# One-hot rows a block ahead of the low parts, two sets of banks for the second products, and a later wait for the last gate store

## The chip, the cores and the metric

One core of a Trainium2 chip runs the kernel. The time is that of one execution on the device in microseconds (us): 2182.56 us, the median of three runs (2181.74 to 2182.63). One more execution was profiled; its own time is 2186.8 us, and the stretch from its first to its last instruction, the span, is 2185.0 us. Times in a trace count from the start of the span.

Engines: TensorE (PE, and PEld for its weight loads), VectorE (DVE), ScalarE (ACT), GpSimd (POOL), and SyncE (SP), which only issues DMAs. Each engine runs its own instructions in their order and waits for the others by semaphores.

## The reference

The program is one layer of an encoder on 512 tokens of width 1024, in float32. Its first half (attention, a convolution, gates, an output projection, a norm) is not touched by the change. The second half, which takes the last two thirds of the time, looks each token up in a table of 16384 single-neuron experts:

```python
q = (hf @ w_q).reshape(T, PEER_HEADS, 2, PEER_DHALF)
scores = jnp.einsum('thpd,pnd->thpn', q, sub_keys)        # 2 x 128 keys for each of 8 heads
sv, si = lax.top_k(scores, 16)
cand = sv[:, :, 0, :, None] + sv[:, :, 1, None, :]
cv, ci = lax.top_k(cand, 16)                               # 16 experts a head: 128 a token
e_idx = si_0[ia] * N_KEYS + si_1[ib]
gates = softmax(cv)
a = einsum('thkd,td->thk', u_tab[e_idx], x)
out = einsum('thk,thkd->td', gelu(a) * gates, v_tab[e_idx])
x = layer_norm(ALPHA * x + (1 + g2) * out, ln2_g, ln2_b)
```

## The kernel before

The experts form a square of 128 x 128 keys. For three of the four token tiles (384 tokens, `TN`) the kernel doesn't gather; it computes all experts: 128 blocks of 128 experts, one block for each first key.
**First products** (`first_product(c)`, L1711 and on). Block c is 24 matrix products of 128 x 384 columns into bank 0 or 1. Its table block `raw` (128 x 1024 floats) is loaded by SP (`load_u`), four buffers. ScalarE copies it to the high part `whi` (L743, in `ahead`, together with the GELU of the block before, L750); three buffers, so the high part of block c+2 waits for the end of block c-1. VectorE subtracts to get the low part `wlo` (`low_u`, L1192), two blocks ahead of its use; for every third block GpSimd does that (L552, `on_pool`). The GELU results `gelz` go to DRAM four blocks at a time (SP), since the weights aren't known yet.

**Beside them.** `select(t)` on VectorE finds the top 16 for tile t; it takes 18 blocks. Then `laying`, 16 blocks a tile, for the three tiles 1 to 3, turns the choices into gates by key: for eight tokens at a time VectorE makes two sets of one-hot rows, `one` (128 slots x 8 tokens x 128 keys each): L1328 compares the first keys with an iota, L1330 the second keys, L1332 multiplies by the softmax weights. TensorE multiplies the two (`token_gates`, L1748, four tokens in a bank, two such steps a block, each ahead of half of the block's products), ScalarE copies the result to `stage` (L766) and every eight steps stores 128 x 4096 floats to DRAM (`gates_by_key`). `one` has two buffers; the rows of step o wait until the gates of step o-2 are done (`gt_mm`). In between VectorE takes the dot products of the gathered tile (`dot`, L1197: `ring` with `x2s`). In the order of the blocks: selection 0 (blocks 0 to 17), selection 1 (to 35), selection 2 (to 53), laying 1 (54 to 69), selection 3 (70 to 87), laying 2 (88 to 103), laying 3 (104 to 119), and a fill stage of eight blocks (120 to 127). In the trace the three laying stages are 779 to 958, 1059 to 1232 and 1233 to 1420 us.

**The fill stage.** Before block 120's part ScalarE waits until all gates are stored (`stage_out`) and issues two loads of gates (`gring`) and three of GELU results (`gback`). From its fifth step on (j = 4) the weights gate x GELU are formed (`weigh`, L1359, VectorE), split (`eh` L812 on ScalarE, `el` L1365 on VectorE), and the rows of the second table are split (`vhi` L824, `vlo` L1371).

**Second products** (`second_product`, L1776 and on). 16 groups of eight blocks; each group once for each half of the 1024 output columns. For each block and each of the three tiles three products of 512 columns are summed in a bank over the eight blocks of the group, and then VectorE adds the sum to `acc` in SBUF (`add`, L1387 and L1389). All half groups use the same banks 2, 3 and 4: the first product of a half group into a bank waits (`pv_add`) until the last sum was read from it. VectorE's low parts `vlo` run three blocks ahead of TensorE, in four buffers. In groups 0 to 5 VectorE also takes dots. Group 6 sets up the gathered tile's weights, by a transpose through bank 5, and in groups 7 to 14 the "quads" (L1802) multiply them with 128 gathered rows of the second table, into banks 6 and 7. The last group writes the gate row of the norm into banks 0 and 1, and VectorE carries out the residual, the norm and the output.

The steps named below are in these functions:

## Time and profile before

| | |
|---|---|
| median of the runs | 2182.56 us |
| the profiled execution, its own time | 2186.8 us |
| its span | 2185.0 us |
| TensorE busy | 1766.1 us, 81% of the span |
| VectorE busy | 1439.6 us, 66% |
| ScalarE busy | 732.3 us, 34% |
| GpSimd busy | 517.4 us, 24% |
| mean granted clock of TensorE | 0.904 of full speed |
| DMA | 441.12 MB, mean 202 GB/s |

The shares are means over stages that have different limits. TensorE has by far the most work, so its idle time is looked at first, by the waits that end it and by stage; then what the engine that it waits for was itself waiting for. "<-" in a row names what was waited for, and the number in brackets at the end of a row of the timeline is the idle time just before it. The granted clock is 1.0 where TensorE runs at 2.4 GHz and 0.5 where it runs at 1.2 GHz. A DMA share is the mean busy share of the 16 DMA engines.

### The profile page before, as it was taken

The page shows a single profiled execution, that of the slowest core. Times are in us where ns is not written, and L with a number is a line of the kernel's source. Part 1 is how long each engine was busy: PE and PEld are TensorE (multiplying, and loading weights), DVE is VectorE, ACT ScalarE, POOL GpSimd, SP SyncE. Part 2 cuts the span into 40 slices and gives each one's busy share as a digit, 9 for nine tenths or more (in the row PEclk, how much of TensorE's full clock was granted, in tenths as well). Part 3 has the DMA queues.
Part 4 walks back from the last instruction along what each step waited for, and adds up shares of the span by engine and source line. Part 5 has one row for each costly group of instructions (what it writes and reads, how often), then busy time and mean ns, then how long its engine had stood idle before and what let it go on. Part 6 is the DMA issues. An engine that isn't in the chain of part 4 may idle for free. (4 is left out here: it accounts for less than half of the span.)

```text
span 2185.0 us, 23650 instructions
## 1 busy us (share of the span) xinstructions
PE 1766.1 (81%) x8496; PEld 1482.6 (68%) x8496; DVE 1439.6 (66%) x2735; ACT 732.3 (34%) x1068; POOL 517.4 (24%) x386
## 2 busy tenths in 40 slices
PE   4997799879989865688665656678988898999985
PEld 3885567669989865688665656677766765566664
DVE  6349998856999954569544444448787654454458
ACT  4433354243323323333233323323333322232232
POOL 1019800020222211112211111123223022343321
PEclk9998899979999988889788778799999998999998
DMA  7242235514465535455335333398888689899982
GB/s 280 68 145 78 78 116 192 174 69 145 165 245 205 176 126 187 149 183 198 121 149 202 141 139 139 130 328 307 288 287 289 217 285 332 311 359 340 348 282 102
DMA packets 177972, 441.12 MB, mean 202 GB/s; under 512 B 15552, under 2 KB 64832, under 8 KB 176320
## 3 DMA queue, kind: packets, MB, share of 16 engines
q1 hardware_dynamic: 78992, 224.62, 29.5%
q0 software_dynamic: 38256, 139.48, 18.1%
q10 hardware_dynamic: 60608, 75.50, 10.1%
q8 instruction: 69, 1.13, 0.2%
q14 instruction: 47, 0.39, 0.0%
HBM read 384.99 MB, written 54.53 MB: 201 GB/s over the span
## 5 line engine op out<-in xcount | busy, mean ns | idle before, releaser
L1516 PE MATMUL bank<-act_hi,whi 128*128 128x384 f32 (+1 forms) x1352 | 504.5, 373 | 39.3 <-DVE wlo L1192 26.1
L1517 PE MATMUL bank<-act_lo,whi 128*128 128x384 f32 (+1 forms) x1352 | 487.2, 360 | 0.0
L1518 PE MATMUL bank<-act_hi,wlo 128*128 128x384 f32 (+1 forms) x1352 | 485.6, 359 | 0.0
L1516 PE MATMUL bank<-vhi,eh 128*128 128x512 f32 x768 | 317.0, 413 | 73.3 <-DVE acc L1389 39.3
L1192 DVE TENSOR_TENSOR wlo<-raw,whi 128x1024 fp32r<-128x1024 f32 x87 | 109.2, 1258 | 321.2 <-ACT whi L743 320.1
L1516 PEld LDWEIGHTS bank<-act_hi,whi 128*128 128x128 f32 x1352 | 270.7, 200 | 60.4 <-DVE wlo L1192 30.3
L1517 PE MATMUL bank<-vlo,eh 128*128 128x512 f32 x768 | 310.1, 404 | 0.0
L1518 PE MATMUL bank<-vhi,el 128*128 128x512 f32 x768 | 308.9, 402 | 0.0
L1371 DVE TENSOR_TENSOR vlo<-vraw,vhi 128x512 fp32r<-128x512 f32 x256 | 175.1, 692 | 200.9 <-ACT vhi L824 174.3
L1748 PE MATMUL bank<-one 128*128 128x128 f32 x768 | 135.3, 333 | 208.7 <-DVE one L1332 208.7
L1517 PEld LDWEIGHTS bank<-act_lo,whi 128*128 128x128 f32 x1352 | 268.9, 199 | 12.3
L1518 PEld LDWEIGHTS bank<-act_hi,wlo 128*128 128x128 f32 x1352 | 266.5, 197 | 13.4
L1748 PEld LDWEIGHTS bank<-one 128*128 128x128 f32 x768 | 124.5, 239 | 219.2 <-DVE one L1332 219.2
L824 ACT ACTIVATE vhi<-vraw 128x512 fp32r<-128x512 f32 x256 | 158.7, 628 | 299.0 <-PE bank L1518 152.5
L544 POOL DMA_INDIRECT ring<-in_u_tab_dram,idxN x128 | 145.1, 1133 | 438.0 <-DVE ring L1197 423.7
L1516 PEld LDWEIGHTS bank<-vhi,eh 128*128 128x128 f32 x768 | 150.3, 196 | 140.5 <-issue 76.3
L552 POOL TENSOR_TENSOR wlo<-raw,whi 128x1024 fp32r<-128x1024 f32 x41 | 100.0, 2439 | 515.8 <-ACT whi L743 515.5
L766 ACT ACTIVATE stage<-bank 128x512 f32<-128x512 f32 x96 | 106.2, 1106 | 341.7 <-PE bank L1748 341.7
L567 POOL DMA_INDIRECT ring<-in_v_tab_dram,idxT x128 | 132.9, 1038 | 328.8 <-PE bank L1802 268.9
L1518 PEld LDWEIGHTS bank<-vhi,el 128*128 128x128 f32 x768 | 150.4, 196 | 33.7
L1517 PEld LDWEIGHTS bank<-vlo,eh 128*128 128x128 f32 x768 | 150.9, 197 | 30.4 <-issue 0.2
L750 ACT ACTIVATE gelz<-bank 128x384 f32<-128x384 f32 x128 | 62.9, 491 | 297.9 <-PE bank L1518 277.6
(222 smaller groups left out, 2359.0 us busy)
## 6 DMA issues: line engine op xcount, KB each, us to landing
raw<-in_u_t_dram SPq DMA_DIRECT2D x128, 512.0 KB
vraw<-in_v_tab_dram SPq DMA_DIRECT2D x256, 256.0 KB
raw<-in_wblk_dram SPq DMA_DIRECT2D x61, 512.0 KB, 4.2
raw<-in_w_modt_dram SPq DMA_DIRECT2D x48, 512.0 KB, 3.5
gelu_ahead<-gelz SPq DMA_DIRECT2D x32, 768.0 KB
gates_by_key<-stage ACTq DMA_DIRECT2D x12, 2048.0 KB
gring<-gates_by_key ACTq DMA_DIRECT2D x32, 768.0 KB
gback<-gelu_ahead ACTq DMA_DIRECT2D x64, 384.0 KB
```

The source lines that it names most:

```text
L544: pool.indirect_dma_start(out=ring[:, j % RING, :], out_offset=None, in_=u_tab, in_offset=bass.IndirectOffsetOnAxis(ap=idxN[:, j:j + 1], a ...
L552: nc.gpsimd.tensor_tensor(wlo[:, c % SPL, :], raw[:, c % RAW, :], whi[:, c % SPL, :].bitcast(F32), ALU.subtract).then_inc(u_lo_pool, 1)
L567: pool.indirect_dma_start(out=ring[:, n % RING, :], out_offset=None, in_=v_tab, in_offset=bass.IndirectOffsetOnAxis(ap=idxT[:, tok:tok + 1 ...
L750: nc.scalar.activation(gelz[:, c % PS, :], bank[c % 2][:, 0:TN], ACT.Gelu_apprx_tanh).then_inc(gel_r, 1)
L766: nc.scalar.activation(stage[:, s, :, t0:t0 + TOK].rearrange("p i t -> p t i"), bank[2 + b % 2][:, :].rearrange("p (t i) -> p t i", t=TOK) ...
L824: nc.scalar.activation(hi_slot, vraw[:, n % VR, :], ACT.Copy).then_inc(v_hi, 1)
L1192: nc.vector.tensor_tensor(wlo[:, c % SPL, :], raw[:, c % RAW, :], whi[:, c % SPL, :].bitcast(F32), ALU.subtract).then_inc(u_lo, 1)
L1371: nc.vector.tensor_tensor(lo_slot, vraw[:, n % VR, :], hi_slot.bitcast(F32), ALU.subtract).then_inc(v_lo, 1)
L1516: mm(o, wh, mh, start=start, stop=False)
L1517: mm(o, wh, ml, start=False, stop=False)
L1518: return mm(o, wl, mh, start=False, stop=stop)
L1748: last = mm(bank[2 + b % 2][:, j * NK:(j + 1) * NK], row[:, 0, i, :], row[:, 1, i, :], start=True, stop=True)
```

## The change

In `laying` on VectorE the one-hot rows of step o+1 are made before the low part of block c0+o+2 (before: those of step o, after it); the rows of the first step are made ahead of the loop. The second half of each group sums in banks 0, 1 and 5 instead of 2, 3 and 4, so that each sum may be read while the next half group runs; the waits `pv_add` look one half group further back, and the first use of banks 0 and 1 waits for the last GELU. The transpose of group 6 goes through bank 6. In the last group the gate row comes one product later and waits for the sums in banks 0 and 1 to be read. The five loads of ScalarE in the fill stage, with the wait for the stores, come after its third step.

```diff
--- before.py
+++ after.py
@@ -350,6 +350,7 @@
             return (whi0, wlo0) if n == 0 else (whi[:, n % SPL, :], wlo[:, n % SPL, :])
 
         Y_BANK = (0, 2, 6, 4)
+        PV_BANK = ((2, 3, 4), (0, 1, 5))
 
 
         TILES = list(range(V0)) + list(range(C0, Y0))
@@ -824,14 +825,15 @@
                 nc.scalar.activation(hi_slot, vraw[:, n % VR, :], ACT.Copy).then_inc(v_hi, 1)
 
 
-            for i in range(2):
-                act.wait_ge(stage_out[i], 16 * (NTB // 2))
-            for i in range(2):
-                load_g(i)
-            for i in range(3):
-                load_back(i)
             for j in range(FILL):
                 ahead(CH - FILL + j)
+                if j == 2:
+                    for i in range(2):
+                        act.wait_ge(stage_out[i], 16 * (NTB // 2))
+                    for i in range(2):
+                        load_g(i)
+                    for i in range(3):
+                        load_back(i)
                 if j >= 4:
                     part_w(j - 4, j - 4)
                 if j >= 5:
@@ -1315,22 +1317,28 @@
                 link(nc.vector.tensor_copy(selT[:, 0:2, :], selI[:]))
                 nc.vector.nop().then_inc(selT_sb, 1)
 
-            def one_hots(t, c0):
+            def one_hots(t, o):
 
                 shape = [P, WIDE, NK]
+                n = P // WIDE * (t - 1) + o
+                need(dve, gt_mm, 2 * n - 2)
+                row = one[o % 2]
+                part = slice(o * WIDE, (o + 1) * WIDE)
+                keys_of = iota[:].unsqueeze(1).broadcast_to(shape)
+                link(nc.vector.tensor_tensor(row[:, 1], selT[:, 0, part].unsqueeze(2).broadcast_to(shape), keys_of,
+                                             ALU.is_equal))
+                nc.vector.tensor_tensor(row[:, 0], selT[:, 1, part].unsqueeze(2).broadcast_to(shape), keys_of,
+                                        ALU.is_equal)
+                nc.vector.tensor_tensor(row[:, 1], row[:, 1], selT[:, 2, part].unsqueeze(2).broadcast_to(shape),
+                                        ALU.mult).then_inc(one_r, 1)
+
+            def laying(t, c0):
+
+                one_hots(t, 0)
                 for o in range(P // WIDE):
+                    if o + 1 < P // WIDE:
+                        one_hots(t, o + 1)
                     low_u(c0 + o + 2)
-                    n = P // WIDE * (t - 1) + o
-                    need(dve, gt_mm, 2 * n - 2)
-                    row = one[o % 2]
-                    part = slice(o * WIDE, (o + 1) * WIDE)
-                    keys_of = iota[:].unsqueeze(1).broadcast_to(shape)
-                    link(nc.vector.tensor_tensor(row[:, 1], selT[:, 0, part].unsqueeze(2).broadcast_to(shape), keys_of,
-                                                 ALU.is_equal))
-                    nc.vector.tensor_tensor(row[:, 0], selT[:, 1, part].unsqueeze(2).broadcast_to(shape), keys_of,
-                                            ALU.is_equal)
-                    nc.vector.tensor_tensor(row[:, 1], row[:, 1], selT[:, 2, part].unsqueeze(2).broadcast_to(shape),
-                                            ALU.mult).then_inc(one_r, 1)
                     dot(next(dots))
 
             low_u(0)
@@ -1343,10 +1351,10 @@
                 select(t, c0)
                 c0 += PRE_S
                 if t > 1:
-                    one_hots(t - 1, c0)
+                    laying(t - 1, c0)
                     c0 += PRE_L
                 transposed(t)
-            one_hots(TT - 1, c0)
+            laying(TT - 1, c0)
 
             def weigh(g, k):
 
@@ -1383,10 +1391,11 @@
                     wait_sum(g, half, t)
                     need(dve, pv_add, 2 * TD * g + TD * half + t - 2 * TD + 1)
                     dst = acc[:, t, half * HALF:(half + 1) * HALF]
+                    src = bank[PV_BANK[half][t]][:, :]
                     if first:
-                        nc.vector.tensor_copy(dst, bank[2 + t][:, :]).then_inc(pv_add, 1)
+                        nc.vector.tensor_copy(dst, src).then_inc(pv_add, 1)
                     else:
-                        nc.vector.tensor_tensor(dst, dst, bank[2 + t][:, :], ALU.add).then_inc(pv_add, 1)
+                        nc.vector.tensor_tensor(dst, dst, src, ALU.add).then_inc(pv_add, 1)
 
             def residual(t, half):
 
@@ -1400,7 +1409,7 @@
 
                 cut = slice(half * HALF, (half + 1) * HALF)
                 wait_sum(NG - 1, half, t)
-                nc.vector.tensor_tensor(acc[:, t, cut], bank[2 + t][:, :], rows2[:, 0, cut],
+                nc.vector.tensor_tensor(acc[:, t, cut], bank[PV_BANK[half][t]][:, :], rows2[:, 0, cut],
                                         ALU.mult).then_inc(pv_add, 1)
 
             def last_sum(t, half):
@@ -1429,7 +1438,7 @@
                     if last and k == 0:
                         dve.wait_ge(w_mul, CH)
                         diagonals(dg2, 40)
-                    if last and k == 2:
+                    if last and k == 3:
                         gate_row(rows2[:, 0, :], 0, 2)
                         dve.wait_ge(x1_in, 32)
                         dve.wait_ge(g_row, 2)
@@ -1465,7 +1474,7 @@
                                                 iota[:, 0:QUAD].unsqueeze(1).broadcast_to([P, QUAD, QUAD]),
                                                 ALU.is_equal)
                         dve.wait_ge(wT_mm, 1)
-                        link(nc.vector.tensor_copy(wT[:], bank[5][:, 0:P]))
+                        link(nc.vector.tensor_copy(wT[:], bank[6][:, 0:P]))
                     if g == W_GROUP and k in (1, 3, 5, 7):
                         part = slice(k // 2 * QUAD, (k // 2 + 1) * QUAD)
                         nc.vector.tensor_tensor(wz[:, part, :], wT[:, part].unsqueeze(2).broadcast_to([P, QUAD, QUAD]),
@@ -1780,11 +1789,13 @@
                 n = half * GR + k
                 pe.wait_ge(v_lo, 16 * g + n + 1)
                 pe.wait_ge(w_lo, GR * g + k + 1)
+                if g == 0 and k == 0 and half == 1:
+                    pe.wait_ge(gel_r, CH)
                 for t in range(TD):
                     if k == 0:
-                        need(pe, pv_add, 2 * TD * g + TD * half + t - TD + 1)
+                        need(pe, pv_add, 2 * TD * (g - 1) + TD * half + t + 1)
                     c = slice(t * P, (t + 1) * P)
-                    last = three(bank[2 + t][:, :], eh[:, k, c], el[:, k, c], vhi[:, n % VR, :], vlo[:, n % VR, :],
+                    last = three(bank[PV_BANK[half][t]][:, :], eh[:, k, c], el[:, k, c], vhi[:, n % VR, :], vlo[:, n % VR, :],
                                  k == 0, k == GR - 1)
                     if k == GR - 1 and t < TD - 1:
                         last.then_inc(pv_mm, 1)
@@ -1808,11 +1819,12 @@
                 at = V_GROUP <= g < V_GROUP + QUAD // 4
                 for k in range(GR):
                     second_product(g, k, 0)
-                    if last and k == 1:
+                    if last and k == 2:
+                        pe.wait_ge(pv_add, 2 * TD * g)
                         gate_row(dg2, 0, 2)
                     if g == W_GROUP and k == 6:
                         pe.wait_ge(own_w, 1)
-                        nc.tensor.transpose(bank[5][:, 0:P], own_a[:], ident[:]).then_inc(wT_mm, 1)
+                        nc.tensor.transpose(bank[6][:, 0:P], own_a[:], ident[:]).then_inc(wT_mm, 1)
                     if at and k % 4 == 3:
                         quad(4 * (g - V_GROUP) + k // 4)
                 if not last:
@@ -1825,14 +1837,15 @@
                 group(g, g == NG - 1)
 
             g = NG - 1
+            pe.wait_ge(g_row, 2)
             for t in range(TD):
                 c = slice(t * P, (t + 1) * P)
-                need(pe, pv_add, 2 * TD * g + TD + t - TD + 1)
+                pe.wait_ge(pv_add, 2 * TD * (g - 1) + TD + t + 1)
                 for k in range(GR):
                     if t == 0:
                         pe.wait_ge(v_lo, 16 * g + GR + k + 1)
                     h, l = v_slot(GR + k, True)
-                    ins = three(bank[2 + t][:, :], eh[:, k, c], el[:, k, c], h, l, k == 0, k == GR - 1)
+                    ins = three(bank[PV_BANK[1][t]][:, :], eh[:, k, c], el[:, k, c], h, l, k == 0, k == GR - 1)
                 ins.then_inc(pv_mm, 1)
```

On VectorE in the first laying stage, from its first step on, before (`one0_86` and `one1_87` are the two buffers of the one-hot rows; `waits u_hi` is the wait for a high part, `waits gt_mm` that for gates; where no `wlo` stands between two steps, GpSimd makes it):

```order
L1328 TENSOR_TENSOR one0_86<-selT_85,iota_109 128x1024
L1330 TENSOR_TENSOR one0_86<-selT_85,iota_109 128x1024 [waits dch]
L1332 TENSOR_TENSOR one0_86<-one0_86,selT_85 128x1024
L1197 SCALAR_TENSOR_TENSOR ring_88,own_a_123<-ring_88,x2s_81 128x1024 [waits ug_in0]
L1192 TENSOR_TENSOR wlo_53<-raw_51,whi_52 128x1024 [waits u_hi]
L1328 TENSOR_TENSOR one1_87<-selT_85,iota_109 128x1024
L1330 TENSOR_TENSOR one1_87<-selT_85,iota_109 128x1024 [waits dch]
L1332 TENSOR_TENSOR one1_87<-one1_87,selT_85 128x1024
L1197 SCALAR_TENSOR_TENSOR ring_88,own_a_123<-ring_88,x2s_81 128x1024 [waits ug_in1]
L1192 TENSOR_TENSOR wlo_53<-raw_51,whi_52 128x1024 [waits u_hi]
L1328 TENSOR_TENSOR one0_86<-selT_85,iota_109 128x1024 [waits gt_mm]
```

And now, at the same place:

```order
L1328 TENSOR_TENSOR one0_86<-selT_85,iota_109 128x1024
L1330 TENSOR_TENSOR one0_86<-selT_85,iota_109 128x1024 [waits dch]
L1332 TENSOR_TENSOR one0_86<-one0_86,selT_85 128x1024
L1328 TENSOR_TENSOR one1_87<-selT_85,iota_109 128x1024
L1330 TENSOR_TENSOR one1_87<-selT_85,iota_109 128x1024 [waits dch]
L1332 TENSOR_TENSOR one1_87<-one1_87,selT_85 128x1024
L1199 SCALAR_TENSOR_TENSOR ring_88,own_a_123<-ring_88,x2s_81 128x1024 [waits ug_in0]
L1328 TENSOR_TENSOR one0_86<-selT_85,iota_109 128x1024 [waits gt_mm]
L1330 TENSOR_TENSOR one0_86<-selT_85,iota_109 128x1024 [waits dch]
L1332 TENSOR_TENSOR one0_86<-one0_86,selT_85 128x1024
L1194 TENSOR_TENSOR wlo_53<-raw_51,whi_52 128x1024 [waits u_hi]
L1199 SCALAR_TENSOR_TENSOR ring_88,own_a_123<-ring_88,x2s_81 128x1024 [waits ug_in1]
```

The second set of rows has moved ahead of the first dot, and each later set ahead of the low part that stood before the set of the step before; the instructions and their number are the same.

On ScalarE in the fill stage, before (`gelz` with L750 is the GELU of a block, `whi` with L743 a high part):

```order
L800 DMA gring<-gates_by_key 128x12x128 [waits stage_out1,stage_out0]
L800 DMA gring<-gates_by_key 128x12x128
L807 DMA gback<-gelu_ahead 128x768 [waits gel_out0] x2
L807 DMA gback<-gelu_ahead 128x768 [waits gel_out1]
L750 ACTIVATE gelz<-bank 128x384 [waits u_mm]
L743 ACTIVATE whi<-raw 128x1024 [waits u_mm,u_in2]
L750 ACTIVATE gelz<-bank 128x384 [waits gel_out0,u_mm]
L743 ACTIVATE whi<-raw 128x1024 [waits u_mm,u_in3]
```

And now:

```order
L751 ACTIVATE gelz<-bank 128x384 [waits u_mm]
L744 ACTIVATE whi<-raw 128x1024 [waits u_mm,u_in0]
L801 DMA gring<-gates_by_key 128x12x128 [waits stage_out1,stage_out0]
L801 DMA gring<-gates_by_key 128x12x128
L808 DMA gback<-gelu_ahead 128x768 [waits gel_out0] x2
L808 DMA gback<-gelu_ahead 128x768 [waits gel_out1]
L751 ACTIVATE gelz<-bank 128x384 [waits u_mm]
L744 ACTIVATE whi<-raw 128x1024 [waits u_mm,u_in1]
```

The five loads stand behind three GELUs and three high parts that followed them before.

## Rows read from the trace of the kernel before

**Rows 1.** Waits, 773 to 1420.1 us: engine, line <- releaser: us, times, longest
```profile
PE bank L1748 <- DVE one L1332: 208.7, 33, 7.4
```

**Rows 2.** Windows: start:end, us, busy of each engine, PEclk, DMA share, GB/s
```profile
779.20:958.50 179.30, 116.13 (x640) 112.93 (x641) 82.97 (x87) 56.40 (x62) 26.50 (x21) 0.80 0.39 139
1058.60:1232.20 173.60, 110.49 (x601) 107.58 (x602) 81.85 (x85) 54.22 (x60) 26.09 (x20) 0.79 0.37 135
1232.60:1420.20 187.60, 118.16 (x641) 114.97 (x642) 90.10 (x98) 57.64 (x64) 26.08 (x20) 0.79 0.40 147
1420.20:1474.80 54.60, 41.94 (x220) 40.21 (x219) 24.86 (x39) 16.19 (x27) 15.76 (x11) 0.93 0.92 328
1474.80:1751.40 276.60, 239.39 (x982) 192.59 (x983) 213.71 (x364) 96.03 (x167) 64.58 (x48) 0.94 0.82 277
1751.40:2126.30 374.90, 345.97 (x1665) 236.24 (x1665) 180.52 (x306) 109.20 (x192) 120.65 (x120) 0.95 0.93 327
```

**Rows 3.** Timeline of VectorE in laying: start us, us, engine, line, operation, [idle before]
```profile
803.63 1.23 DVE L1192 TENSOR_TENSOR wlo<-raw,whi 128x1024 fp32r<-128x1024 f32 x1 [8.44 <-ACT whi L743]
804.77 1.22 DVE L1328 TENSOR_TENSOR one<-selT,iota 128x1024 f32<-128x1024 f32 x1
...
808.30 1.22 DVE L1197 SCALAR_TENSOR_TENSOR ring<-ring,x2s 128x1024 f32<-128x1024 f32 x1
...
809.44 1.22 DVE L1328 TENSOR_TENSOR one<-selT,iota 128x1024 f32<-128x1024 f32 x1
...
1060.07 1.23 DVE L1192 TENSOR_TENSOR wlo<-raw,whi 128x1024 fp32r<-128x1024 f32 x1 [8.04 <-ACT whi L743]
```

**Rows 4.** Timeline of TensorE: the gate products, eight each, two steps a block
```profile
779.23 2.08 PE L1748 MATMUL bank<-one 128*128 128x128 f32 x8 [5.52 <-DVE one L1332]
...
784.65 1.05 PE L1748 MATMUL bank<-one 128*128 128x128 f32 x8
...
812.99 1.05 PE L1748 MATMUL bank<-one 128*128 128x128 f32 x8
...
815.96 1.05 PE L1748 MATMUL bank<-one 128*128 128x128 f32 x8
...
1238.89 2.08 PE L1748 MATMUL bank<-one 128*128 128x128 f32 x8 [6.34 <-DVE one L1332]
```

**Rows 5.** Timeline of ScalarE in laying
```profile
814.08 1.10 ACT L766 ACTIVATE stage<-bank 128x512 f32<-128x512 f32 x1 [2.44 <-PE bank L1748]
816.16 0.49 ACT L750 ACTIVATE gelz<-bank 128x384 f32<-128x384 f32 x1 [0.98 <-PE bank L1518]
816.55 1.05 ACT L743 ACTIVATE whi<-raw 128x1024 fp32r<-128x1024 f32 x1
```

**Rows 6.** Timelines of GpSimd and VectorE where they meet
```profile
775.47 2.62 POOL L552 TENSOR_TENSOR wlo<-raw,whi 128x1024 fp32r<-128x1024 f32 x1
...
775.81 3.36 DVE L1332 TENSOR_TENSOR one<-one,selT 128x1024 f32<-128x1024 f32 x1
```

**Rows 7.** Timelines of ScalarE's DMA issue and of TensorE in the fill stage
```profile
1427.06 3.94 ACTq L807 DMA_DIRECT2D gback<-gelu_ahead  x3
...
1431.68 0.66 PE L1516 MATMUL bank<-act_hi,whi 128*128 128x384 f32 x1 [7.16 <-ACT gelz L750]
```

**Rows 8.** Waits, 1474.8 to 1751.4 us
```profile
DVE vlo L1371 <- ACT vhi L824: 33.1, 38, 3.3
...
PE bank L1516 <- DVE acc L1389: 23.9, 10, 3.2
...
PE bank L1516 <- DVE acc L1387: 5.8, 2, 4.0
```

**Rows 9.** Waits, 1751.4 to 2130 us, and one DMA issue of ScalarE
```profile
PE bank L1516 <- DVE vlo L1371: 20.9, 5, 5.3
...
PE bank L1516 <- DVE acc L1389: 15.4, 4, 7.5
...
1797.77 6.57 ACTq L807 DMA_DIRECT2D gback<-gelu_ahead  x1
```

## The prediction

> **What bounds the kernel now.** I read the waits first, then busy time by stretch, then the order of time on the engines that meet there. The table of waits between 773 and 1420.1 us has one entry that matters for TensorE: the token gates (L1748) waited 208.7 us, 33 times, for the one-hot rows (L1332) [rows 1]. So in the three laying stages TensorE is the engine waited for by ScalarE, and VectorE is what holds TensorE. VectorE itself is not full there, so the stages run in a ring and not at the pace of any engine. The windows say it: laying takes 179.3, 173.6 and 187.6 us, TensorE is busy 116.1, 110.5 and 118.2 us of it, VectorE 83.0, 81.9 and 90.1, at a granted clock near 0.8 and a DMA share near 0.4 [rows 2]. (The second window begins where TensorE's wait for the first one-hot rows begins, the third with the transposes of the values that it needs.)
>
> The ring can be followed in time. ScalarE takes the GELU of a finished block at 816.16 and makes the next high part at 816.55 [rows 5]. VectorE makes the low part (803.63), and only then the one-hot rows (804.77 to 808.30), then a dot [rows 3]. TensorE can't begin its block before the one-hot rows are there. GELU 0.4 + high part 1.05 + low part 1.14 + one-hot rows 3.53 are 6.1 us, and the wait on record is 6.3 (5.52 to 6.34 in the first waits of the stages) [rows 4, 5]. Only where GpSimd makes the low part (every third block) is there no such wait, since then VectorE goes straight on, at 809.44. After a wait TensorE runs at the lower of its two levels (1.2 instead of 2.4 GHz) for a while: the first half block after 779.23 took 5.42 us to 784.65, one at the full level 2.97 (812.99 to 815.96) [rows 4].
>
> **The laying stages, 48 blocks.** Now the rows of block o+1 are made before the low part of block o+2. They need only the gates of block o-1, which are done in the middle of that block; they are wanted when block o+1 begins. The low part that comes behind them is wanted a block later still. Put on one clock, with TensorE beginning block o-1 at 0 and a block taking 2 x 2.97 = 5.94: its second gates are read by 4.0; one-hot rows of o+1 from 4.0 to 7.6; high part of o+2 at 5.9 + 1.5 = 7.4; low part 7.6 to 8.7; dot to 9.9. The rows are wanted at 11.9 and the low part at 17.8. So neither is late, by 4.3 and 9.1 us, and what is left is throughput. TensorE: 5.94 a block. VectorE: 1.14 + 3.53 + 1.14 = 5.81, or 4.67 where GpSimd makes the low part. ScalarE: GELU 0.4, high part 1.05, two gate copies of 1.1 are 3.65 [rows 5]. TensorE is the bound, closely followed by VectorE.
> - First stage: 16 x 5.94 = 95.0, and 2.4 for the slow start behind the 5.52 us that stay (VectorE is full in the selection before it): 97.4 instead of 179.3, saves 81.9.
> - Second: the first wait goes too, since VectorE is idle 8.04 us ahead of 1060.07 and can make two sets there [rows 3]: 95.0 instead of 173.6, saves 78.6.
> - Third: it starts right behind the transposes of the values. Of 6.34 us the low part's 1.14 goes, 5.2 stay: 102.6 instead of 187.6, saves 85.0.
>
> Sum 245.5. That asks for more DMA: 139 GB/s x 179.3/97.4 = 256 GB/s, by share 0.39 x 1.84 = 0.72 [rows 2]. The queue order of SP is unchanged, but it carries the 512-KB loads of raw (128 x 1024 floats) behind a 768-KB store of gelz every fourth block, and blocks come almost twice as fast. I take 4 us off for single late loads: **241.5**.
>
> The shared port has a price of its own. Where GpSimd's subtraction (2.62 us at 775.47) met VectorE's multiplication (775.81), that took 3.36 instead of 1.22, 2.14 more [rows 6]. Before, most subtractions fell into VectorE's idle time; now VectorE is hardly ever idle. Three blocks cost VectorE 5.81 + 5.81 + 4.67 + 2.14 = 18.43, TensorE 17.82. The excess, 0.6 a triple or 3.3 us in a stage, is inside the 4.3 us that the rows are ahead, so I charge nothing. The Trainium skill (SBUF — State Buffer, "Who interferes with whom") says that a VectorE instruction with two SBUF inputs and a GpSimd instruction that reads SBUF exclude each other for a whole instruction. All five VectorE operations of a block have two such inputs, so by that rule every one of the 16 subtractions is paid; the row at 775.81 agrees with it.
>
> **The last gate store waited for later.** ScalarE now stands still behind block 119: the wait for the store and five DMA issues (three of them 3.94 us from 1427.06) precede the GELU that TensorE waits for, 7.16 us, to 1431.68 [rows 7]. Behind ahead(122) the store has long landed. The issues (5 to 6.6 us for five, going by the 3.94 for three) then delay one high part by 2.5 to 4 us, and its low part is wanted more than a block later. That saves 7.2 + 2 for the slow start. But the weights' first product (at j = 4) now comes some 10 us behind the issue of its operands instead of 20, with the DMA engines at 0.92 of their time [rows 2]. Bounds: -3 (a stall as long as one issue group, less what is hidden) and +9.4. I take **7**, near the upper end, since TensorE has a block in hand there.
>
> **Two sets of sum banks.** Groups 0 to 6 take 276.6 us [rows 2]. TensorE waits 23.9 + 5.8 = 29.7 us for additions in 12 waits [rows 8]; with a second set these waits go. What is late next is VectorE: its order is the same, its low parts run only three products ahead of TensorE, and it is busy 213.7 us of the stretch and waits inside the chain multiply, high part, low part (0.6 a time). All that it could gain are the 33.1 us in which it waits for vhi [rows 8]. So the bounds are 0 and 30. DMA share 0.82 would become 0.88 to 0.92. I take **18**, a bit over half: both engines have to gain it together, and they hand over three products at a time.
>
> Groups 7 to 14 run at a DMA share of 0.93 [rows 2]. There TensorE waits 15.4 us for additions, 20.9 for vlo [rows 9], and the latter stand behind a ScalarE that sat 6.57 us in one DMA issue, 1797.77 [rows 9]. That isn't touched; an addition's wait that goes is mostly taken up by the next of those. Bounds 0 and 22 (15.4 and 4 slow starts of 1.6); I take **5**.
>
> The rest is nothing: bank 6 in the place of 5 for one transpose is unused there (the quads start behind it); gel_r at the first use of banks 0 and 1 was reached a half group ago; in the last group the gate row comes one product later with the same instructions on VectorE, whose chain sets the end either way. 0, bounds -2 and +1.
>
> **Sum.** 241.5 + 7 + 18 + 5 = 271.5. From the profiled execution's 2186.8 (span 2185.0) that is 1915.3; the median of the runs, 2182.6, is 4.2 lower, so 1911.
>
> **Rivals.**
> - *The feed becomes the bound in laying* (0.14). For: behind each 768-KB store the next load is 2 blocks (11.9 us) ahead of its use, with a gate store of 2048 KB (128 x 4096 floats) and 512-KB gathers beside it: 5.2 MB in the worst case, at the 328 GB/s of the fill stage [rows 2] nearly 16 us. 12 such places, 3.6 us each and a slow start of 1.6: 62 us, 1973. Against: a share of 0.72 on the mean, and only 3 of the 4 blocks are loaded late. The Trainium skill (DMA: Bandwidth & Descriptors, "Queues, rings and completion order") has the DMA engines take turns between queue rows packet by packet, so that the load would have at least a third of the rate; by that the 1.3 MB of the store and the load would be through in about 12 us and the stall near nothing. No run here shows the turns.
> - *The shared port sets laying's pace* (0.10), the skill's rule above at full price and the rows' lead used up: 16 x 0.6 = 10 us, 1921.
> - *The second products gain nothing* (0.07), VectorE's chain and DMA taking all: 241.5 + 7 give 1934.
> - *The wait moves from the one-hot rows to the low part* (0.02): the change would not do what it says. It needs the low part 9 us later than reckoned; the other parts alone (7 + 18 + 5) give 2153.
> - *Slower* (0.01): every VectorE operation of laying stretched as at 775.81, by GpSimd's gathers too. It decides from the point where a block costs VectorE more than the present mean, 542/48 = 11.3 us; three of five operations stretched by 2.14 give 12.2, 48 x 0.9 = 43 us more: 2226. Against: the operations of rows 3 took 1.22 us each; the stretched one stands beside a subtraction, and of those there is one in three blocks.
>
> **How the numbers follow.** The forecast has 0.66. Its own range is 1890 to 1935 (30, 22 and 9.4 instead of 18, 5 and 7 below; half of the second part's gain lost and a few late loads above). The range that I give is 1885 to 1960: it takes in the port, the second products and a partly late feed. Two runs of this kernel tell a difference of over 0.2% (4.4 us). Faster 0.98, same 0.01, slower 0.01.
>
> **What would show it.** Right: in laying about 6 us a block, the wait of L1748 for the one-hot rows down to some 11 us in 2 or 3 times, granted clock near 1.0, DMA share near 0.7; no wait for "acc" before the last group, but waits for vlo in its place; TensorE not idle at the start of the fill stage. Wrong: waits of ScalarE's whi for raw in laying (the feed), VectorE at 0.98 of laying with TensorE waiting under 1 us each time (the port), or laying still above 7 us a block.

## The result and the profile after

The changed kernel took 1925.37 us (median of 4 runs, 1920.16 to 1927.09), the kernel before beside it 2182.15 (4 runs, 2181.11 to 2182.63): 0.882 of the time, 95% interval 0.8801 to 0.8839. The forecast was 1911 us, its range 1885 to 1960. The profiled execution took 1926.98 us, its span is 1925.2, 259.8 less than before. One of the runs below, of the kernel with all edits together, took 2796.5 us at a mean granted clock of 0.558 and is left out of its ratio; nothing here tells why.

First the waits of TensorE over the three laying stages of the changed kernel (781 to 1172 us); this answers to [rows 1].

```profile
PE bank L1757 <- DVE one L1332: 17.4, 5, 6.0
...
DVE one L1328 <- PE bank L1757: 6.0, 6, 1.2
...
ACT whi L744 <- DMA raw<-in_u_t_dram: 2.3, 2, 1.3
```

The wait for the one-hot rows fell from 208.7 us in 33 times to 17.4 in 5. Now it is VectorE that waits (6.0 us in all) for gates that TensorE has yet to take, and ScalarE waited only 2.3 us for loads of raw: the feed kept up.

Next the windows of the changed kernel that answer to [rows 2]: laying one to three, fill stage, groups 0 to 6 up to the first quad, first to last quad (start:end, us, busy of each engine, PEclk, DMA share, GB/s).

```profile
781.70:878.50 96.80, 96.77 (x640) 96.60 (x641) 89.99 (x87) 56.34 (x62) 37.32 (x21) 0.98 0.73 257
969.80:1068.60 98.80, 98.42 (x641) 97.94 (x642) 93.25 (x88) 56.50 (x62) 38.68 (x21) 0.97 0.68 251
1074.20:1171.90 97.70, 97.36 (x640) 97.04 (x641) 94.13 (x90) 56.59 (x62) 36.64 (x20) 0.98 0.72 270
1172.00:1225.20 53.20, 41.63 (x221) 39.90 (x219) 24.87 (x39) 16.98 (x29) 14.62 (x11) 0.90 0.98 347
1225.20:1497.80 272.60, 248.11 (x1022) 199.50 (x1024) 217.29 (x372) 96.38 (x171) 59.84 (x48) 0.94 0.83 286
1497.80:1863.20 365.40, 333.21 (x1613) 226.27 (x1612) 173.01 (x294) 105.61 (x186) 119.33 (x120) 0.95 0.93 329
```

In laying TensorE is busy for the whole window, its granted clock went from 0.8 to 0.98, and the DMA share from 0.39 to about 0.7, as forecast. Read from start to start of the stages, the 259.8 us are:

| part | before | after | saved | predicted |
|---|---|---|---|---|
| up to the wait ahead of laying one | 773.7 | 776.3 | -2.6 | 0 |
| laying one | 179.3 | 96.8 | 82.5 | 81.9 |
| laying two, with its first wait | 188.7 | 104.8 | 83.9 | 78.6 |
| laying three, with its first wait | 187.6 | 103.0 | 84.6 | 85.0 |
| fill stage | 54.6 | 53.2 | 1.4 | 7 |
| groups 0 to 6 (up to the first quad) | 287.6 | 272.6 | 15.0 | 18 |
| groups 7 to 14 (first to last quad) | 362.0 | 365.5 | -3.5 | 5 |
| tail | 60.6 | 62.0 | -1.4 | 0 |

What is not in the table (the wait ahead of laying one, and selection 3) took about 91 us in both. The two rows of the groups part at the first quad, which stands four products behind the start of group 7; the prediction's window ended at that start (1751.4 us before, 1481.0 now). Parted there, groups 0 to 6 went from 276.6 to 255.8 us and the rest up to the last quad from 373.0 to 382.3. The difference is one wait: the 7.50 us for an addition that TensorE had ahead of 1751.43 are gone, and 1.03 and 4.55 us for low parts have come inside the first four products of group 7. In either parting the two rows together gained 11.5 us, where the forecast had 23.

A steady block of laying can be read off TensorE's gate products and VectorE's order (timelines of the changed kernel, start us, us, engine, line, operation).

```profile
1008.38 1.05 PE L1757 MATMUL bank<-one 128*128 128x128 f32 x8
1011.35 1.05 PE L1757 MATMUL bank<-one 128*128 128x128 f32 x8
1014.33 1.05 PE L1757 MATMUL bank<-one 128*128 128x128 f32 x8
...
1008.07 1.21 DVE L1328 TENSOR_TENSOR one<-selT,iota 128x1024 f32<-128x1024 f32 x1
1009.32 1.23 DVE L1330 TENSOR_TENSOR one<-selT,iota 128x1024 f32<-128x1024 f32 x1
1010.46 1.22 DVE L1332 TENSOR_TENSOR one<-one,selT 128x1024 f32<-128x1024 f32 x1
1011.60 1.22 DVE L1194 TENSOR_TENSOR wlo<-raw,whi 128x1024 fp32r<-128x1024 f32 x1
1012.73 1.22 DVE L1199 SCALAR_TENSOR_TENSOR ring<-ring,x2s 128x1024 f32<-128x1024 f32 x1
...
1013.88 1.22 DVE L1328 TENSOR_TENSOR one<-selT,iota 128x1024 f32<-128x1024 f32 x1
```

Half a block is 2.97 us on TensorE, a block 5.95; VectorE's round is 5.81, from 1008.07 to 1013.88. Both are the numbers of the forecast.

In the groups, the waits of the changed kernel from 1225.2 to 1497.8 us, and from 1497.8 to 1863.2; they answer to [rows 8] and [rows 9].

```profile
PE bank L1525 <- DVE vlo L1379: 31.0, 9, 6.5
...
DVE vlo L1379 <- ACT vhi L825: 23.2, 29, 3.1
...
PE bank L1525 <- DVE vlo L1379: 32.0, 6, 7.1
...
ACT vhi L825 <- issue: 44.9, 9, 7.8
```

TensorE waits for no addition any more. The last row is ScalarE standing in load issues, 44.9 us in nine times.

### The profile page after: what moved, and what is told of

Same layout as the page of the kernel before. It is cut to its first block and busy times, and to the rows that moved or that the text cites. A ratio compares the mean times of both kernels' runs of the same rounds, so it can differ in the third digit from the quotient of the medians.

```text
span 1925.2 us, 23651 instructions
## 1 busy us (share of the span) xinstructions
PE 1706.1 (89%) x8496; PEld 1431.3 (74%) x8496; DVE 1460.8 (76%) x2735; ACT 730.2 (38%) x1068; POOL 543.0 (28%) x386
## 3 DMA queue, kind: packets, MB, share of 16 engines
q10 hardware_dynamic: 60608, 75.50, 11.5%
## 5 line engine op out<-in xcount | busy, mean ns | idle before, releaser
L1525 PE MATMUL bank<-act_hi,whi 128*128 128x384 f32 (+1 forms) x1352 | 491.1, 363 | 38.2 <-DVE wlo L1194 26.6
L1526 PE MATMUL bank<-act_lo,whi 128*128 128x384 f32 (+1 forms) x1352 | 477.7, 353 | 0.0
L1527 PE MATMUL bank<-act_hi,wlo 128*128 128x384 f32 (+1 forms) x1352 | 477.6, 353 | 0.0
L1525 PE MATMUL bank<-vhi,eh 128*128 128x512 f32 x768 | 316.8, 413 | 66.0 <-DVE vlo L1379 65.8
L1525 PEld LDWEIGHTS bank<-act_hi,whi 128*128 128x128 f32 x1352 | 260.2, 192 | 58.7 <-DVE wlo L1194 30.1
L545 POOL DMA_INDIRECT ring<-in_u_tab_dram,idxN x128 | 166.6, 1302 | 389.9 <-DVE ring L1199 378.0
L1526 PEld LDWEIGHTS bank<-act_lo,whi 128*128 128x128 f32 x1352 | 260.0, 192 | 12.4
L1527 PEld LDWEIGHTS bank<-act_hi,wlo 128*128 128x128 f32 x1352 | 259.3, 192 | 13.2
L553 POOL TENSOR_TENSOR wlo<-raw,whi 128x1024 fp32r<-128x1024 f32 x41 | 106.4, 2594 | 277.9 <-ACT whi L744 277.6
L1199 DVE SCALAR_TENSOR_TENSOR ring<-ring,x2s 128x1024 f32<-128x1024 f32 x128 | 164.4, 1286 | 0.4
L1194 DVE TENSOR_TENSOR wlo<-raw,whi 128x1024 fp32r<-128x1024 f32 x87 | 109.1, 1256 | 48.5 <-ACT whi L744 47.6
L893 DVE TENSOR_TENSOR wlo<-raw,whi 128x1024 fp32r<-128x1024 f32 x61 | 80.0, 1311 | 77.9 <-ACT whi L586 77.9
```

Of the source, the lines that this page charges most:

```text
L545: pool.indirect_dma_start(out=ring[:, j % RING, :], out_offset=None, in_=u_tab, in_offset=bass.IndirectOffsetOnAxis(ap=idxN[:, j:j + 1], a ...
L553: nc.gpsimd.tensor_tensor(wlo[:, c % SPL, :], raw[:, c % RAW, :], whi[:, c % SPL, :].bitcast(F32), ALU.subtract).then_inc(u_lo_pool, 1)
L893: nc.vector.tensor_tensor(low[:, :], raw[:, s % RAW, :], high[:, :].bitcast(F32), ALU.subtract).then_inc(raw_free, 1)
L1194: nc.vector.tensor_tensor(wlo[:, c % SPL, :], raw[:, c % RAW, :], whi[:, c % SPL, :].bitcast(F32), ALU.subtract).then_inc(u_lo, 1)
L1199: nc.vector.scalar_tensor_tensor(out=ring[:, j % RING, :], in0=ring[:, j % RING, :], scalar=1.0, in1=x2s[:], op0=ALU.mult, op1=ALU.mult, a ...
L1525: mm(o, wh, mh, start=start, stop=False)
```

## The experiments

All were timed beside the kernel before on the same chip; its median there was 2182 to 2187 us. The changed kernel's 1925.4 (ratio 0.882, interval 0.8801 to 0.8839) is the measure for those that build on it; of a difference of less than about 0.3% (6 us) the time tells little, and the traces are read. A trace is one execution, and stages in which two kernels are alike differ in it too: the first gates of laying one come between 778.8 and 782.6 us in the kernels that change nothing ahead of them, and first to last quad take 361.3 to 368.3 us in the kernels with the same instructions there.

### Which part brought the time

**The order in laying alone**, on the kernel before:

```diff
+                one_hots(t, 0)
                 for o in range(P // WIDE):
+                    if o + 1 < P // WIDE:
+                        one_hots(t, o + 1)
                     low_u(c0 + o + 2)
-                    (the rows of step o)
                     dot(next(dots))
```

> The kernel before with the new order of laying alone. Theory A (the laying stages give nearly all): the three stages take 97, 105 and 103 us as in the changed kernel, instead of 184.8, 188.7 and 187.6 (waits for the first rows included), so about 251 us less than before: 1931 us, 1927 to 1936. Rival B (the stages gain only because the other edits take load off VectorE or DMA): over 1945 us. The waits of the gate products for the one-hot rows: about 17 us in all, by A.

Measured: 1938.6 us (1929.57 to 1939.64), ratio 0.8865, interval 0.8842 to 0.8888. That is 2.6 us above theory A's range and below B's. In its trace TensorE's first gates of the three stages wait 5.45, 6.02 and 5.20 us, 16.7 in all, as theory A has it.

**All but that**, the changed kernel with laying in the old order:

```diff
-                one_hots(t, 0)
                 for o in range(P // WIDE):
-                    if o + 1 < P // WIDE:
-                        one_hots(t, o + 1)
                     low_u(c0 + o + 2)
+                    (the rows of step o)
```

> The changed kernel with laying in the old order: banks, fill stage and last group are as changed. Theory A: these edits are worth what the two traces differ by behind the laying stages, 1.4 (fill) + 15.0 (groups 0 to 6) - 3.5 (groups 7 to 14) - 1.4 (end) = 11.5 us: 2171 us, 2167 to 2175. The prediction's terms 7 + 18 + 5 would give 30 us: 2152.

Measured: 2171.8 us (2170.77 to 2173.49), ratio 0.9943, interval 0.9925 to 0.9962. Theory A. Against 2183.8 the order alone is worth 245.2 us, the rest alone 12.0, together 257.2; both at once brought 256.8 (2182.15 less 1925.37). So the parts add. The laying sum of the forecast (241.5) holds within 4 us, and the other terms (30 together) came to 12.

**The fill stage's loads at their old place:**

```diff
+            for i in range(2): load_g(i)
+            for i in range(3): load_back(i)
             for j in range(FILL):
-                if j == 2: (the same five loads)
```

> The changed kernel with the five loads and the wait for the gate stores ahead of the fill stage again. Theory A (the stall only moved from block 121 to block 124, since the five issues take 11.1 us when the DMA queues are full): 0 to 3 us slower than the changed kernel, 1926 to 1928. The prediction's term would give 7 us: 1932.

Measured: 1927.64 us (1920.06 to 1930.31), ratio 0.8814, interval 0.8792 to 0.8837. Not to be told from the changed kernel; the 7 us of the forecast are not there. Why, these rows of the changed kernel show (timelines of ScalarE's queue and of TensorE; they answer to [rows 7]).

```profile
1181.94 5.93 ACTq L801 DMA_DIRECT2D gring<-gates_by_key  x2
1187.91 5.21 ACTq L808 DMA_DIRECT2D gback<-gelu_ahead  x3
1193.17 0.49 ACT L751 ACTIVATE gelz<-bank 128x384 f32<-128x384 f32 x1 [10.23 <-issue]
...
1193.81 0.66 PE L1525 MATMUL bank<-act_hi,whi 128*128 128x384 f32 x1 [5.05 <-ACT gelz L751]
```

The five issues held ScalarE for 11.1 us where the forecast had 5 to 6.6. That is more than the block that TensorE had in hand, so the same wait came back later, 5.05 us instead of 7.16. It is the place that made them long: at the old place the same five took 1.17 + 3.94 us before the change (1425.85 and 1427.06), and in this experiment, with everything else as changed,

```profile
1175.63 1.17 ACTq L801 DMA_DIRECT2D gring<-gates_by_key  x2
1176.84 3.99 ACTq L808 DMA_DIRECT2D gback<-gelu_ahead  x3
```

In the changed kernel they come three blocks later and meet SyncE's traffic (a gelz store at 1172.66 and four 512-KB loads of raw issued from 1173.08 on, ahead of the five here; behind them in the experiment, from 1181.81 on): the DMA share is 1.00 from 1172 to 1182 us and 1.03 from 1182 to 1188, against 0.83 from 1172 to 1182 in the experiment. That the full DMA engines are what lengthens an issue fits these numbers; it isn't shown apart from the place.

**One set of sum banks** (shown are the lines of the sums; the reads, the transpose and the last group go back with them):

```diff
-        PV_BANK = ((2, 3, 4), (0, 1, 5))
 ...
-                        need(pe, pv_add, 2 * TD * (g - 1) + TD * half + t + 1)
+                        need(pe, pv_add, 2 * TD * g + TD * half + t - TD + 1)
 ...
-                    last = three(bank[PV_BANK[half][t]][:, :], ...
+                    last = three(bank[2 + t][:, :], ...
```

> The changed kernel with one set of sum banks (and the last group's edits with it) as before. Theory A: the additions' waits come back and the second products lose what they had gained, 15.0 - 3.5 - 1.4 = 10 us: 1935, 1931 to 1940. Rival: the prediction's 18 + 5 = 23 us: 1948. The group period in groups 1 to 5 back from 38.0 to about 40 us.

Measured: 1930.84 us (1928.54 to 1936.05), ratio 0.8839, interval 0.882 to 0.8858. That is at the lower edge of theory A (1931 to 1940) and far from the 1948 of the forecast's terms. The intervals meet, so the time alone doesn't tell this kernel from the changed one, but the traces tell where the bank sets act. From the first second product to the first quad they take 304.8 us here and 285.4 in the changed kernel; from there to the last quad 358.6 and 365.5. (The order in laying alone, which has one set too: 299.6 and 363.4.) So the second set is worth 14 to 19 us up to the first quad. Behind it the 2 to 7 us that it seems to cost lie within what like kernels differ by (361.3 to 368.3): there is surely no gain, and whether there is a cost stays open.

### What limits the groups

In the changed kernel a group of the first seven takes 38.0 us, and TensorE stands once in each, near its beginning; two of these waits:

```profile
1262.69 0.80 PE L1525 MATMUL bank<-vhi,eh 128*128 128x512 f32 x1 [3.04 <-DVE vlo L1379]
1300.63 0.80 PE L1525 MATMUL bank<-vhi,eh 128*128 128x512 f32 x1 [3.44 <-DVE vlo L1379]
```

What VectorE and ScalarE did ahead of the one at 1300.63:

```profile
1295.09 1.88 DVE L1398 TENSOR_TENSOR acc<-acc,bank 128x512 f32<-128x512 f32 x3
1296.88 0.55 DVE L1373 TENSOR_TENSOR el<-wf,eh 128x384 fp32r<-128x384 f32 x1
1297.35 0.55 DVE L1367 TENSOR_TENSOR wf<-gback,gring 128x384 f32<-128x384 f32 x1
1298.49 0.56 DVE L1373 TENSOR_TENSOR el<-wf,eh 128x384 fp32r<-128x384 f32 x1 [0.59 <-ACT eh L813]
1299.88 0.69 DVE L1379 TENSOR_TENSOR vlo<-vraw,vhi 128x512 fp32r<-128x512 f32 x1 [0.84 <-ACT vhi L825]
...
1297.93 0.52 ACT L813 ACTIVATE eh<-wf 128x384 fp32r<-128x384 f32 x1 [2.21 <-DVE wf L1367]
1297.94 0.38 ACTq L801 DMA_DIRECT2D gring<-gates_by_key  x1
1298.41 0.71 ACTq L808 DMA_DIRECT2D gback<-gelu_ahead  x1
1299.22 2.19 ACT L825 ACTIVATE vhi<-vraw 128x512 fp32r<-128x512 f32 x4 [0.77 <-issue]
```

Three additions, two weighings handed to ScalarE and back (0.59 us of idleness each), then two load issues on ScalarE, and only then the high part for which VectorE's low part and so TensorE wait.

**VectorE's load taken away:** dots of groups 0 to 5 over 8 columns.

```diff
-                        dot(next(dots))
+                        dot(next(dots), w=8)
```

> The changed kernel with the dot products of groups 0 to 5 taken over 8 columns instead of the whole row of 2048; the gathers that feed them stay as they are, so most of these dot products is left out and nothing else. In the changed kernel a group of the second half takes 38.0 us (TensorE's waits for the last low part at 1262.69, 1300.63, 1338.62 us), and the question is what sets these 38.0. A (VectorE's chain of low parts, dot product, one-hot sets and adds is full): with about 2.2 us of dot product a step gone, a group falls to where TensorE ends last, at most 35.5 us, and the six groups save 15 us or more: 1905 to 1912 us. B (the loads through the DMA engines, or their issues on ScalarE and GpSimd, set the group): 37.5 to 38.0 us a group and 1922 to 1928 us.

Measured: 1916.92 us (1907.41 to 1918.73), ratio 0.8752, interval 0.8727 to 0.8777. VectorE's busy time between 1260 and 1444 us fell from 150.9 to 115.7 us, but the group only from 38.0 to 36.7 (waits from 1259.70 to 1443.18 in five groups) and the stretch to the first quad from 285.4 to 278.8. Neither theory. (A dot takes 1.22 us on a row of 1024, less than the 2.2 on 2048 that the expectation counts.) VectorE isn't full as an engine, and the loads aren't the limit either, since the next experiment gets far below this with all of them. The chain at the group's start above has no dot in it, and stayed.

**The low parts of the weights one step later**, so that VectorE doesn't wait for ScalarE's answer; ScalarE's high parts of the weights go one step later too, so that it doesn't wait for VectorE's product (ScalarE first, then VectorE):

```diff
-                    if k and not last:
-                        part_w(GR * g + GR + k - 1, k - 1)
+                    if k > 1 and not last:
+                        part_w(GR * g + GR + k - 2, k - 2)
+                if not last:
+                    part_w(GR * g + GR + GR - 2, GR - 2)
 ...
-                        if k < GR - 1:
-                            low_w(g + 1, k - 1)
+                        if k > 1:
+                            low_w(g + 1, k - 2)
```

> The changed kernel with the low part of a chunk in the groups taken one step later behind its high part, on VectorE, so that VectorE no longer waits 0.59 us for ScalarE's high part at each step of a group. A (VectorE's chain sets the group of 38.0 us): 14 waits of 0.59 us, 8.3 us a group at most, of which TensorE's own time lets a part through; 2 to 3 us a group in the first seven groups: 1905 to 1914 us. B (the loads set the group): 1923 to 1928 us. C (the last low part of a group, on which TensorE waits, comes later by the shift): 1930 us or more.

Measured: 1901.68 us (1899.41 to 1903.52), ratio 0.8695, interval 0.8681 to 0.871. Theory A, and 3.3 us more than it gave: the stretch to the first quad is 259.0 us, 26.4 less. VectorE's wait for the weights' high part was

```profile
DVE el L1373 <- ACT eh L813: 28.9, 49, 0.6
```

in the changed kernel (1225 to 1498 us; 31.9 us in 54 times from 1212.3 on, the like stretch), and in this one (1212.5 to 1471.5)

```profile
DVE el L1375 <- ACT eh L813: 7.1, 12, 0.6
```

That is 24.8 us less, close to the gain. ScalarE's own wait for the product (eh <- wf) fell as well, from 84.9 to 33.4 us; both moved in one edit, so the run tells what the hand-over costs and not which of its two sides.

Behind the first quad nothing was gained (367.9 against 365.5).

**ScalarE's load issues at the group's start put behind the third high part** (`loads_behind` holds the two loads that `part_w` issued):

```diff
-                        part_w(GR * g + GR - 1, GR - 1)
+                        part_w(GR * g + GR - 1, GR - 1, loads=False)
                     part_v(g, k + 3, last)
+                    if k == 2:
+                        loads_behind(GR * g + GR - 1)
```

> The changed kernel with ScalarE's load issues that stood behind the first high part of a group put behind the third. In the groups with stores of gates (7 to 14) TensorE waits 4.0 to 7.1 us for the last low part, and ScalarE stands in load issues before it. A (the issues block ScalarE's high parts and through them VectorE's low parts): the waits of these eight groups fall by 2 to 4 us each: 1900 to 1912 us. B (ScalarE is only blocked later by the same time, and the chain is as long as before): 1922 to 1930 us. C (loads come too late for the next group): over 1930 us.

Measured: 1888.06 us (1882.23 to 1891.7), ratio 0.8628, interval 0.8608 to 0.8647. Theory A in its kind, and larger: first to last quad take 336.4 us, 29.1 less. Another 4.7 came ahead of the first quad. It had been the issue that set TensorE's wait there. The issues are as long as before (8.43 us at 1773.10 in this kernel), but they stand behind the high parts that TensorE waits for. In the changed kernel they stood ahead of them (ScalarE, then TensorE):

```profile
1532.54 0.38 ACTq L801 DMA_DIRECT2D gring<-gates_by_key  x1
1533.01 7.19 ACTq L808 DMA_DIRECT2D gback<-gelu_ahead  x1
1540.30 2.19 ACT L825 ACTIVATE vhi<-vraw 128x512 fp32r<-128x512 f32 x4 [7.24 <-issue]
...
1541.71 0.80 PE L1525 MATMUL bank<-vhi,eh 128*128 128x512 f32 x1 [4.68 <-DVE vlo L1379]
```

**Every load of ScalarE in the groups apart from the others** (`gates_behind` and `gelu_behind` issue the gate load and the GELU load that belong to a block; in the fill stage they stay together):

```diff
                     part_v(g, k + 3, last)
+                    if k == 1: gelu_behind(GR * g + 5)
+                    if k == 3: gates_behind(GR * g + 7)
+                    if k == 6: gelu_behind(GR * g + 7)
 ...
                         part_w(GR * g + GR + k - 1, k - 1)
+                        if k == 2: gelu_behind(GR * g + 9)
+                        if k == 4: gates_behind(GR * g + 11)
+                        if k == 7: gelu_behind(GR * g + 11)
```

> The changed kernel with every gate load and every gelu load that ScalarE issues in the groups set apart from each other: none directly behind another, two of the three first-half issues behind the second, fourth and seventh high part. In the changed kernel an issue directly behind a gate load takes 4 to 8 us (7.58 us at 1804.89, 4.32 us at 1822.29) and one by itself 0.3 to 0.4 us. Putting the first-half loads behind the third high part had brought 37 us. A (an issue takes long only because the one before it of the same queue still waits for room): the issues fall to 0.4 us and so do TensorE's waits for low parts: 1865 to 1885 us. B (moving them off the start of the group was all that counted, the issues stay at 4 to 8 us): 1884 to 1892 us. C (the loads land too late): over 1895 us, with waits of VectorE for the DMA.

Measured: 1877.27 us (1876.15 to 1879.35), ratio 0.8595, interval 0.8571 to 0.8619. Theory A. ScalarE's issues in this kernel, about the place where a 7.58 us issue had stood, and the window of groups 7 to 14:

```profile
1774.44 0.33 ACTq L808 DMA_DIRECT2D gback<-gelu_ahead  x1
...
1777.34 0.33 ACTq L808 DMA_DIRECT2D gback<-gelu_ahead  x1
...
1781.45 0.38 ACTq L801 DMA_DIRECT2D gring<-gates_by_key  x1
...
1487.60:1813.50 325.90, 321.39 (x1615) 220.95 (x1614) 174.10 (x294) 106.22 (x186) 126.92 (x120) 0.99 1.02 372
```

No issue in the groups is over 2 us any more, where the changed kernel had ten of them, 3.2 to 7.8 us each. TensorE is busy 321.4 of 325.9 us; and the DMA engines, which looked full at a share of 0.93 and 329 GB/s, moved 372 GB/s. TensorE's waits for low parts aren't all gone: 28.2 us in 14 times are left from the first second product to the last quad. (The first quad comes 7.9 us sooner as well, after 277.6 us instead of 285.5.)

### Laying and the fill stage

**Low parts of laying's blocks all on VectorE** (the expectation names the second and third stage; blocks 56 to 71 are those of the first, so the edit covers all three):

```diff
-            return c > 3 and c % 3 == 2
+            return c > 3 and c % 3 == 2 and not (56 <= c < 72 or 90 <= c < 122)
```

> The changed kernel with the low parts of the blocks of the second and third laying stage (chunks 56 to 71 and 90 to 121) all on VectorE, where GpSimd takes every third. A (the rival of the shared port: a low part on GpSimd keeps VectorE out for about 2.1 us, 16 times, and VectorE has that time on the path): the two stages get shorter by up to 10 us where VectorE's own low part costs less than the exclusion does: 1913 to 1921 us. B (TensorE at 5.94 us a block is the bound of these stages and covers the exclusions): no change by more than 2 us, 1923 to 1927 us, and with it TensorE's waits for the one-hot rows stay near 17.4 us in five places. C (VectorE runs full there and the low parts moved to it push it over TensorE's time): 1930 us or more.

Measured: 1915.34 us (1909.94 to 1919.42), ratio 0.8759, interval 0.8736 to 0.8782. The collision is real. In the changed kernel the multiplication that TensorE's first gates of laying wait for stood beside GpSimd's subtraction (2.62 us from 777.97):

```profile
778.31 3.36 DVE L1332 TENSOR_TENSOR one<-one,selT 128x1024 f32<-128x1024 f32 x1
```

and without it

```profile
775.76 1.22 DVE L1332 TENSOR_TENSOR one<-one,selT 128x1024 f32<-128x1024 f32 x1
```

TensorE's wait ahead of it fell from 5.45 to 3.31 us. Nor is it a single case: in the changed kernel each of the three laying stages has five VectorE operations that took 2.1 to 3.4 us beside a subtraction of GpSimd instead of 1.22, about 9.7 us a stage, such as this (GpSimd, then VectorE)

```profile
1021.99 2.42 POOL L553 TENSOR_TENSOR wlo<-raw,whi 128x1024 fp32r<-128x1024 f32 x1 [6.08 <-ACT whi L744]
...
1022.08 3.40 DVE L1332 TENSOR_TENSOR one<-one,selT 128x1024 f32<-128x1024 f32 x1
```

Before the change there was none behind the first gates of a stage. But from the first gates of laying two to the last of laying three only 2.0 us went (199.2 to 197.2) when the subtractions left GpSimd, so VectorE paid for nearly every collision and TensorE for nearly none, as forecast: the time falls in theory A's range, the stages follow B. 2.1 + 2.0 us are in stages that the edit touches. The rest of the 10 us is in the selection before and the groups behind (282.6 for 285.4, 361.8 for 365.5), which it doesn't touch; each of these differences is no larger than that between like kernels, but what moved the median by more than the 4.1 us is open.

**The first one-hot set of laying one and two ahead of the selection's end** (that is, before the low parts that stood there; the expectation calls the two stages the second and third):

```diff
                 last.then_inc(sel_r, 1)
+                if t > 1:
+                    one_hots(t - 1, 0)
```

> The changed kernel with the first one-hot set of the second and third laying stage made on VectorE ahead of the last part of the selection (for them the prediction had said that a wait would go that stayed: TensorE stood 6.01 and 5.20 us there). A (the set only changes its place on a VectorE that is full up to that point, and what it displaces is on the path): within 2 us of the changed kernel, the two waits shorter but the selection longer by as much. B (it runs in a gap of the selection): the two waits fall by 2.3 us each, 1919 to 1922 us.

Measured: 1916.45 us (1912.94 to 1918.97), ratio 0.8778, interval 0.8754 to 0.8803. Theory B in its kind, and 2.6 us below its range: the 5.45 us ahead of laying one are gone, with 1.57 left ahead of its second block (the collision of 778.31 has moved there), and the 6.01 fell to 3.74 us, since a low part and a dot now stand behind the rows and not ahead of them. The gain is all ahead of laying one (its first gates come at 772.27 instead of 781.73); about 3 of these 9.5 us also came in kernels that change nothing there.

**The fill stage's loads over three steps:**

```diff
-                if j == 2: (five loads)
+                if j == 1: load_g(0)
+                if 1 <= j < 4: load_back(j - 1)
+                if j == 3: load_g(1)
```

> The changed kernel with the five loads that ScalarE issues in the filling stage spread over three steps: one and one at the first, one at the second, two at the third, in place of five at once. In the changed kernel the five issues take 5.93 and 5.21 us on ScalarE and TensorE waits 5.05 us there. A (an issue stands only behind another one of its queue that is still being taken in, so spread issues cost little): TensorE's wait for the gelu at L751 goes, and 3 to 5 us with it: 1920 to 1923 us. B (each issue costs its time wherever it stands): the wait stays or is split, 1924 to 1928 us. Against the scatter of this kernel (1920 to 1927 us) the waits are to be read, not the time alone.

Measured: 1919.74 us (1915.91 to 1924.4), ratio 0.8786, interval 0.876 to 0.8813. Inconclusive in time. In the trace TensorE's wait is 3.34 instead of 5.05 us, and one issue is left that takes

```profile
1179.47 8.94 ACTq L808 DMA_DIRECT2D gback<-gelu_ahead  x1
```

directly behind the gate load of the same step, which fits what the groups showed.

**All of it together:**

> The edits of the five kernels that came out below the changed kernel in one: loads set apart in the groups (alone 1877.3 us), low parts one step behind in the groups (alone 1901.7), laying blocks' low parts all on VectorE (alone 1915.3), first one-hot sets early (alone 1916.5), and the filling stage's five loads each in a step of its own, the gate loads at the first and fourth, the gelu loads at the second, third and fifth (in another split alone 1919.7). A (the parts lie in different stages, so they add): 48 + about 14 (of the 24 of the low parts one step behind, those of groups 0 to 6, two us each) + 4 + 9 + 4 = 79 us below the changed kernel, 1838 to 1852 us. B (in the groups only one of two limits can be moved: with the loads apart the low parts are no limit any more, or the other way round): 1855 to 1868 us. No issue of ScalarE over 2 us should be left in either case.

Measured: 1850.09 us (median of six, the one named with the result among them; the other five 1847.53 to 1852.03), ratio 0.8448, interval 0.8433 to 0.8464. Theory A, near its upper end. TensorE's waits in this kernel that answer to those above:

```profile
PE bank L1551 <- DVE vlo L1405: 26.0, 18, 4.8
...
PE bank L1783 <- DVE one L1357: 9.7, 3, 5.2
```

65.8 and 17.4 us in the changed kernel. One statement of the expectation failed: two issues over 2 us are left, both in the fill stage (6.38 us at 1170.50, 3.9 us behind the end of a gate load's issue; 2.11 at 1188.71). And the stretch to the first quad took 266.6 us where the low parts one step later had reached 259.0 alone; why is open.

## Why the prediction was right, and where it was off

**Laying.** Right in mechanism and size: 251.0 us by the stages, less the 2.6 lost ahead of them, against 245.5, and 245.2 by the experiment that has this edit alone. Blocks of 5.95 us, granted clock 0.98, the rows never late in the steady state; the collisions with GpSimd cost VectorE some 9.7 us a stage, and its lead covered them. The 4 us taken off for late loads were not needed (2.3 us of waits on ScalarE, beside other work).

One step failed in reading, though its number came near: "the first wait goes too, since VectorE is idle 8.04 us ahead of 1060.07 and can make two sets there". The row at 1060.07 stands before the second block of that stage, not before the first. The stage's first wait, 7.42 us at 1050.93, was missed; what stands before it on VectorE is the end of the selection, two low parts and a dot, and so 6.01 us of it stayed (3.74 where the rows were put ahead of them). Timed from the right start the stage was 188.7 us long, not 173.6. The saving then is 188.7 less 104.8 = 83.9 and not 78.6.

**The fill stage.** The failed step: "The issues (5 to 6.6 us for five, going by the 3.94 for three) then delay one high part by 2.5 to 4 us". They took 11.1. As a reading of the old place the price was right: five issues took 1.17 + 3.94 there, and 1.17 + 3.99 with all other edits in. What failed is that the price was taken along to another place. Behind block 122 the two gate loads took 5.93 us and the three others 5.21, at a DMA share of 1.03. So TensorE's wait only moved, from the second block of the stage to the fifth. The result, 1.4, is inside the bounds of -3 to +9.4.

**Groups 0 to 6.** The wait for additions went, and that for vlo took its place, as told. 15.0 us up to the first quad (14 to 19 by the experiments), 20.8 up to the start of group 7, against 18. The reason for what wasn't gained was only partly right: it was less VectorE's load (most of the dots' work gone: 6.6 us) than the order of its hand-overs with ScalarE (one step later: 26.4 us).

**Groups 7 to 14.** The gain of 5 isn't there: -3.5 from first to last quad, -9.3 from the start of group 7. The 15.4 us of waits for additions that the term starts from were 7.9 behind the first quad; the others are the 7.50 at 1751.43, which stand at the end of the window that the term for groups 0 to 6 had used. No wait for additions was left, but the vlo waits grew from 20.9 us in 5 times to 32.0 in 6. The forecast had seen the 6.57 us issue and then read the DMA share of 0.93 as the bound. The issue was the bound: with the issues apart the stretch took 325.9 us at a share of 1.02.

**The rivals.** The feed as bound (1973) is refuted: 2.3 us of waits. The shared port (1921) landed nearer to the time than the forecast, but for another reason: its price was 10 us in laying, and laying came out as forecast, while the 14 us between 1911 and 1925 are in the fill stage (5.6), the groups (11.5), the tail (1.4) and the time ahead of laying (2.6), less the 9.5 us that laying brought beyond its 241.5, and 2.6 us because the profiled execution lay only 1.6 above the median this time, not 4.2. That the forecast came as near as that is in part luck, since laying's surplus paid for a good part of what the other terms lacked. Taking the subtractions off GpSimd bought 4 us in the stages concerned. The rule of the Trainium skill (SBUF — State Buffer, "Who interferes with whom") agrees with the trace: 3.36 for 1.22 us in the single collision, and 15 such operations in the three stages. VectorE paid for each; what the time paid is another matter, and here VectorE's lead covered nearly all. Second products at nothing (1934) is off too: all edits but the order brought 12.0 us (interval 8 to 16), though that is nearer to nothing than to the forecast's 30. A moved wait (2153) and slower (2226) are refuted by the table above.
